# Attention outputs of seven tiles kept in device memory, and one output projection over all channels in the last tile

## Chip, cores and metric

The kernel runs on one core of a Trainium2 chip. The time is the device time of one execution in microseconds (us), from the first to the last instruction of the program with what lies around it. A core has five engines with a queue each: TensorE (PE), VectorE (DVE), ScalarE (ACT), GpSimd (POOL) and SyncE (SP). They run in order and wait for each other by semaphores. DMA queues move data between device memory and the on-chip memory (SBUF). Matmul results go to PSUM, eight banks of 512 f32 per partition.

## What is computed

One inference step of a two-layer encoder for 1024 prompt tokens and 8 x 16 sample tokens (1152 columns in all, `TOK`), model width 1024, in f32. Layer 0 mixes with differential attention (A, 4 heads) and windowed attention (B, 8 heads), layer 1 with a chunk band of 16 heads (C). Each mixer is followed by a gated conv FFN. What the change touches is the last line of each mixer, cut to it here:

```python
def even_mixer(h, pos, lam, lam_init, g_sub, sinks, w_in, w_out, cache):
    qa, ka, va, qb, kb, vb = split_even(h @ w_in)
    ...
    oa = rmsnorm(oa, g_sub) * (1 - lam_init)
    y = jnp.concatenate([oa.reshape(b, t, A_WIDTH), ob], axis=-1) @ w_out
    ...
def odd_mixer(h, pos, table, w_in, w_out, cache):
    ...
    return o @ w_out, (k_new, v_new)
```

and in the caller the gated residual: `x = x + gate * y`. `w_out` is 1024 x 1024, so y is a sum over 1024 attention channels.

## The kernel before

Activations lie transposed, channels on partitions: `xT` (the residual stream), `h` (normalized input, 8 slices of 128 channels x 1152) and `hl`, its low part. Every f32 product is made of three passes: high by high (f32r), high by low and low by high (bf16). `mm3` issues them for one block of columns, `mm9` for all 1152 columns in three blocks (`COLS`: 512, 512, 128), nine matmuls.

`attention` runs once per layer. It walks over **tiles** of 128 attention channels: tiles 0 to 3 are the heads of A and 4 to 7 those of B in layer 0, and 8 to 15 are C in layer 1. `T0` is a layer's first tile. A tile has 8 query blocks (units 0 to 7, with two score passes z), a drain (unit 8) and two groups of sample streams with cached keys.

`tile_steps` writes out the order of a tile as one list of steps, and every engine's `do` goes through the same list and issues its part of each step:
- KT, VT (transposes of k and v), CQ, CK, VS (splits of q, k, v into high and low), then for each unit S (scores, maxima, exponentials), T (transpose of the probabilities), V (product with v), N, O (the finished output, written by ACT to `actr` and by DVE to `actl`).
- F steps are filler for PE: one F is one `mm9` of the q, k or v projection of the *next* tile, eight of them per projection, 24 for three. A tile of B whose successor shares its keys has only the eight of q. The numbers in `body` are slots, and F steps are spread over them in proportion.
- OUT steps, eight a tile: step n multiplies `actr`/`actl` of the tile *before* by block n of `w_out` (`out_piece`, L1404) into banks 0 to 2, and DVE adds it, times the gate, to `xT` (`out_evac`, L1768; per step two of L1777, then L1783 and L1787). The next piece waits for that (`out_evac` semaphore), since it uses the same banks. They stand in units 0 and 1, which get no F steps. The last tile of a layer has OUT steps and no F; its own eight pieces come behind it.
- W splits weights: they come through `ring`, two slots of 128 x 1024. SP loads a chunk (`ring.load`, L162) once its slot's low part is made; ACT makes the high part (L169) and DVE the low part (L174) at a W step, which stands behind the end of a projection and prepares the chunk after next. The W behind v stands at the very end of a tile, ahead of the next VT.

In layer 0 all tiles are written out. In layer 1 the six tiles 9 to 14 are one loop (`Fori`, L1018). `act_free` lets ACT write `actr` again once the pieces of the tile before are evacuated. Behind a tile's KT and VT, PE also uses banks 3 and 4 (scores), 5 and 6 (transposes) and 7.

## Time and profile before

| | |
|---|---|
| median of 3 runs | 4500.71 us (4496.37 to 4506.84) |
| profiled execution, its own time | 4492.89 us |
| its span | 4491.3 us |
| mean granted TensorE clock | 0.899 |
| attention, layer 0 / layer 1 (first q copy to the last output) | 308.6 to 1361.6 / 2371.1 to 3515.0 us |
| HBM read / written | 250.80 / 51.56 MB |

A row of the windows view gives, for a stretch of the span, the busy time of each engine with the number of its instructions, the mean granted TensorE clock (1.00 is 2.4 GHz, 0.50 is 1.2 GHz), and the DMA engines' share and rate. A row of the timeline gives start, duration, engine, line, result and operands, and in brackets the idle time before it and who ended it. The busy time of PE counts modelled ends of matmuls and is not its peak rate. The windows of the tiles are cut where ACT starts to copy q (L1503, step CQ); an "opening" reaches from there to the first write of `actr`.

### The profile page before, as it was taken

The numbers are of one execution on the slowest core, as the hardware profiler recorded it, in microseconds if no ns is written. First come the engines' busy times: TensorE is split into PE (matmuls) and PEld (weight loads), VectorE is DVE, ScalarE is ACT, GpSimd is POOL, SyncE is SP. The second block draws the span as 40 slices with busy tenths as digits, with TensorE's granted clock in tenths as the row PEclk, the third lists the DMA queues.
The fourth block names the chain that finished last, engine by engine and source line by source line (L and its number), as shares of the span: only waits on it lengthen the run. The fifth ranks groups of instructions, "written<-read, shape, count | busy, mean of one in ns | idle before, by whom it ended". The sixth has DMA issues, their size and how long they took to land. (4 is left out here: it accounts for less than half of the span.)

```text
span 4491.3 us, 58536 instructions
## 1 busy us (share of the span) xinstructions
PE 3841.7 (86%) x21708; PEld 2211.7 (49%) x22097; DVE 2302.5 (51%) x3748; ACT 1365.6 (30%) x2652; POOL 466.2 (10%) x997
## 2 busy tenths in 40 slices
PE   6868887887867999999968888888888799999996
PEld 3535455544443555555535555555555355555553
DVE  4554555545446555555544555455544555555554
ACT  5533333333333122121223333333332321212212
POOL 0002122212110000000001111011110000000000
PEclk9887888878758999999988889999985799999998
DMA  7612122201001111111002232122321111111111
GB/s 297 239 46 58 41 60 73 58 23 44 21 17 43 39 43 43 38 43 40 27 24 86 86 98 91 50 79 93 98 76 36 39 43 43 39 39 43 43 34 43
DMA packets 200133, 277.97 MB, mean 62 GB/s; under 512 B 23984, under 2 KB 157721, under 8 KB 199286
## 3 DMA queue, kind: packets, MB, share of 16 engines
q1 hardware_dynamic: 170422, 164.42, 11.3%
q0 software_dynamic: 29504, 110.77, 8.2%
q8 instruction: 133, 2.18, 0.2%
q14 instruction: 74, 0.61, 0.0%
HBM read 250.80 MB, written 51.56 MB: 67 GB/s over the span
## 5 line engine op out<-in xcount | busy, mean ns | idle before, releaser
L95 PE MATMUL psum<-h,ffn_high 128*128 128x512 f32 (+1 forms) x2112 | 1036.9, 531 | 47.5 <-DVE hl L464 47.5
L97 PE MATMUL psum<-hl,ffn_high 128*128 128x512 bf16 (+1 forms) x2028 | 616.8, 337 | 0.0
L99 PE MATMUL psum<-h,ffn_low 128*128 128x512 bf16 (+1 forms) x2066 | 579.3, 332 | 2.9
L95 PE MATMUL psum<-actr,ffn_high 128*128 128x512 f32 (+1 forms) x1056 | 515.6, 528 | 56.5 <-DVE xT L482 40.8
L95 PEld LDWEIGHTS psum<-h,ffn_high 128*128 128x128 f32 x2112 | 409.7, 194 | 134.2 <-issue 43.6
L97 PEld LDWEIGHTS psum<-hl,ffn_high 128*128 128x128 bf16 x2112 | 206.4, 98 | 432.3 <-issue 373.4
L774 DVE TENSOR_SCALAR y<-u,cvT 128x1168 f32<-128x1168 f32 x88 | 78.2, 888 | 529.9 <-ACT u L725 529.9
L95 PE MATMUL psum<-h,attC_high 128*128 128x512 f32 (+1 forms) x576 | 288.4, 540 | 37.1 <-DVE hl L464 23.2
L97 PE MATMUL psum<-actl,ffn_high 128*128 128x512 bf16 (+1 forms) x1012 | 308.1, 337 | 0.0
L99 PE MATMUL psum<-actr,ffn_low 128*128 128x512 bf16 (+1 forms) x1034 | 290.3, 332 | 1.5
L95 PE MATMUL psum<-h,attAB_high 128*128 128x512 f32 (+1 forms) x480 | 262.9, 587 | 31.5 <-DVE hl L464 23.2
L169 ACT CAST ffn_high<-ffn_raw 128x1024 fp32r<-128x1024 f32 x132 | 138.8, 1054 | 478.0 <-PE psum L99 478.0
L95 PEld LDWEIGHTS psum<-actr,ffn_high 128*128 128x128 f32 x1056 | 205.2, 194 | 104.4 <-DVE xT L482 50.8
L719 ACT COPY u<-psum 128x1024 f32<-128x1024 f32 x88 | 89.3, 1014 | 546.9 <-PE psum L99 546.5
L482 DVE SCALAR_TENSOR_TENSOR xT<-psum,mod,xT 128x1024 f32<-128x1024 f32 x176 | 224.8, 1277 | 0.0
L1579 ACT ACTIVATE E_C<-psum,st_C 128x640 f32<-128x640 f32 (+3 forms) x144 | 97.3, 676 | 415.2 <-DVE st_C L1740 415.2
L97 PEld LDWEIGHTS psum<-actl,ffn_high 128*128 128x128 bf16 x1056 | 103.4, 98 | 212.6 <-issue 180.5
L1662 DVE TENSOR_TENSOR Wl_C<-psum,W_C 128x640 bf16<-128x640 f32 (+3 forms) x144 | 97.5, 677 | 196.6 <-ACT W_C L1533 196.0
L1579 ACT ACTIVATE E_AB<-psum,st_AB 128x256 f32<-128x256 f32 (+5 forms) x144 | 87.1, 605 | 361.3 <-DVE st_AB L1740 361.3
L593 POOL COPY so<-u 128x2 f32<-128x2 f32 x88 | 17.6, 200 | 1666.8 <-ACT u L720 1666.8
L1777 DVE SCALAR_TENSOR_TENSOR xT<-psum,mod,xT 128x512 f32<-128x512 f32 x256 | 181.7, 745 | 16.0 <-PE psum L87 15.3
L99 PEld LDWEIGHTS psum<-h,ffn_low 128*128 128x128 bf16 x2112 | 182.0, 100 | 0.0
(406 smaller groups left out, 8517.5 us busy)
## 6 DMA issues: line engine op xcount, KB each, us to landing
ada_raw<-in_ada_w SPq DMA_DIRECT2D x48, 1024.0 KB, 8.2
ffn_raw<-in_w_up SPq DMA_DIRECT2D x88, 512.0 KB, 4.0
ffn_raw<-in_w_down SPq DMA_DIRECT2D x44, 512.0 KB, 3.4
raw_C<-in_cache_c_k POOLq DMA_DIRECT2D x64, 256.0 KB, 6.2
raw_C<-in_cache_c_v POOLq DMA_DIRECT2D x64, 256.0 KB, 3.5
out_ck_s<-in_cache_c_k POOLq DMA_DIRECT2D x8, 1984.0 KB, 9.5
out_cv_s<-in_cache_c_v POOLq DMA_DIRECT2D x8, 1984.0 KB, 15.2
attC_raw<-in_w_in_odd SPq DMA_DIRECT2D x24, 512.0 KB, 3.9
```

The lines of the kernel that those rows point to most:

```text
L95: return pe.matmul(out, w, x[:, lo:hi], start=first and start, stop=last and stop, skip_group_check=True)
L97: return pe.matmul(out, top(w), xl[:, lo:hi], start=first and start, stop=last and stop, skip_group_check=True)
L99: return pe.matmul(out, wl, top(x[:, lo:hi]), start=first and start, stop=last and stop, skip_group_check=True)
L169: act.copy(self.w[s][:, :], self.raw[c % self.raws][:, :]).then_inc(self.high[s], 1)
L482: return dve.scalar_tensor_tensor(out=G.xT[:, n, 0:SEQ], in0=y[:, 0:SEQ], scalar=G.mod[:, a, 16 + n, 0:1], in1=G.xT[:, n, 0:SEQ], op0=ALU. ...
L593: pool.tensor_copy(so[:, 2 * g + j, 0:2], U[g][:, SEQ:SEQ + 2])
L719: act.copy(U[gate][:, 2:2 + SEQ], ps[:, 3 * gate:3 * gate + 2, :].rearrange("p b n -> p (b n)"))
L774: ch.then(dve.tensor_scalar(y[:, 0:n], u[:, 2:2 + n], cv[:, l, 2, bass.ds(f, 1)], cv[:, l, 3, bass.ds(f, 1)], ALU.mult, ALU.add))
L1579: i_ = act.activation(E[:, off:off + wd], s_banks[:, 0:wd], ACT.Exp, bias=nm[:, z:z + 1], scale=SCALE, accum_out=sm[:, z:z + 1])
L1662: i_ = dve.tensor_tensor(Wl[:, w0:w0 + wn], t_banks[:, 0:wn], W[:, w0:w0 + wn].bitcast(F32), ALU.subtract)
L1777: i_ = dve.scalar_tensor_tensor(out=x, in0=y, scalar=G.mod[:, a, 16 + n, 0:1], in1=x, op0=ALU.mult, op1=ALU.add)
```

## The change

- The OUT steps are gone. Once a tile of a layer (but the last) is done, SP writes `actr` and `actl` to device memory (`spill`: 128 x 1152 f32 and the same in bf16, two DMAs). It stands in SP's list behind the load of the q chunk of the tile after, and waits for the last `act_low` of its tile. ACT may write `actr` again once it has left (`act_free`).
- In the last tile (`TL`), when the last projection of the layer is done and `h` is free, SP reads the seven spilled tiles back into `h[:, 0..6]` and `hl[:, 0..6]` (`restore`, 14 DMAs). The last tile writes its own output to `h[:, 7]` (`act_of`).
- P steps (n, k), 56 of them, are the filler of the last tile from unit 3 on: `mm9` of slice k of `h` with block (k, n) of `w_out`, accumulated over k = 0 to 6 in banks 0 to 2. `w_out` comes by columns for these, eight loads. After k = 6 DVE adds the sum to `xT` by `residual`, the helper of the FFN (three instructions over 1152 columns); the next n waits for that.
- Behind the tile eight `mm9` with slice 7 and rows 896 to 1023 of `w_out` go to banks 0 to 2 and 3 to 5 by turns.
- The loop over tiles 9 to 14 is written out like the rest.
- `rtmp` gets its own SBUF place.

The diff, cut to its core:

```diff
-def tile_steps(kind, fill, out, keys):
+def tile_steps(kind, fill, last, keys):
...
-    steps = [("KT",), ("VT",), ("CQ",)] + outs[0:1] + [("CK",)] + outs[1:2] + [("VS",)] if keys else [("CQ",)] + outs[0:2]
+    steps = [("KT",), ("VT",), ("CQ",), ("CK",), ("VS",)] if keys else [("CQ",)]
...
-        one, two = ((outs[2:4], outs[4:5]), (outs[5:6], outs[6:8]))[u] if u < 2 and out else ([4], [4])
+        one, two = ([0], [0]) if last and u < 3 else ([4], [4])
...
+    todo = [("P", n, k) for n in range(KT) for k in range(KT - 1)] if last else \
+        [("F", name, k) for name in fill for k in range(KT)]
...
@@ sync, in do @@
-                if s == ("OUT", 0):
-                    row = (T - 1 - (8 if odd else 0)) * P
-                    ring.load(sp, c, w_out[bass.ds(row, P), :], turns)
+                if what == "P" and s[2] == KT - 2:
+                    ring.load(sp, c, w_out.rearrange("(k p) n -> p k n", p=P)[:, :, s[1] * P:(s[1] + 1) * P], 0,
+                              ("p (k n) -> p k n", dict(k=KT)))
+                    if s[1] == 1:
+                        spill(T - 1)
+                        restore()
...
                         ring.load(sp, c, src, turns, ("p (k n) -> p k n", dict(k=KT)))
+                    if s[1] == "q" and T > T0:
+                        spill(T - 1)
+
+            def spill(T):
+
+                t = T - T0
+                if T == TL - 1:
+                    sp.wait_ge(S.spilled, sb_ + 32 * t)
+                sp.wait_ge(S.act_low, un(T, UNITS - 1))
+                sp.dma_start(G.act_high_dram[t], actr[:, :].bitcast(F32)).then_inc(S.spilled, 16)
+                sp.dma_start(G.act_low_dram[t], actl[:, :]).then_inc(S.spilled, 16)
+
+            def restore():
+
+                ring.done(sp, cb + tiles[-1][3] - 1)
+                for t in range(7):
+                    if t == 6:
+                        sp.wait_ge(S.restored, sb_ + 32 * 6)
+                        sp.wait_ge(S.spilled, sb_ + 32 * 7)
+                    sp.dma_start(h[:, t, :].bitcast(F32), G.act_high_dram[t]).then_inc(S.restored, 16)
+                    sp.dma_start(hl[:, t, :], G.act_low_dram[t]).then_inc(S.restored, 16)
...
@@ tensor, in do @@
+                elif what == "P":
+                    j, k = s[1:]
+                    w, wl = ring.ready(pe, c) if k == 0 else (ring.w[c % 2][:, :], ring.wl[c % 2][:, :])
+                    if j == k == 0:
+                        pe.wait_ge(S.v_rows, n + 1)
+                        pe.wait_ge(S.q_evac, T + 1)
+                        pe.wait_ge(S.restored, sb_ + 32 * 6)
+                    elif k == 0:
+                        pe.wait_ge(S.out_evac, 2 * KT * odd + j)
+                    elif j == 0 and k == KT - 2:
+                        pe.wait_ge(S.restored, sb_ + 32 * 7)
+                    mm = mm9(pe, ps, 0, w[:, k * P:(k + 1) * P], wl[:, k * P:(k + 1) * P],
+                             h[:, k, :], hl[:, k, :], k == 0, k == KT - 2)
...
@@ scalar @@
             def act_free(T, c, turns):
-                act.wait_ge(S.out_evac, 3 * KT * T)
+                if T < TL:
+                    act.wait_ge(S.spilled, sb_ + 32 * (T - T0))
...
@@ vector, in do @@
-                elif what == "OUT":
-                    out_evac(T - 1, s[1], c, turns)
+                elif what == "P" and s[2] == KT - 2:
+                    ring.done(dve, c)
+                    residual(dve, ch, S, G, s[1], a, 0, rtmp[:, s[1] % 2, :]).then_inc(S.out_evac, 1)
```

**How the order moves.** First PE at the start of tile 9, the second tile of layer 1, before the change (L1292 the transposes of v, `actr_C`/`actl_C` the output of tile 8, the last row the first score):

```order
L1292 MATMUL psum<-consts,f_v_C 128x128 [waits v_evac]
L1292 MATMUL psum<-consts,f_v_C 128x128 x8
...
L85 MATMUL psum<-actr_C,attC_high 128x512 [waits v_rows,act_low]
L86 MATMUL psum<-actl_C,attC_high 128x512
L87 MATMUL psum<-actr_C,attC_low 128x512
...
L85 MATMUL psum<-actr_C,attC_high 128x512 [waits out_evac]
...
L85 MATMUL psum<-k_C,q_C 128x128 [waits exps]
```

and with the change, at the same place (`h` and `attC_high`: the first group of the projection for tile 10):

```order
L1313 MATMUL psum<-consts,f_v_C 128x128 [waits v_evac]
L1313 MATMUL psum<-consts,f_v_C 128x128 x8
L85 MATMUL psum<-k_C,q_C 128x128 [waits exps,k_low,q_low]
L86 MATMUL psum<-kl_C,q_C 128x128
L87 MATMUL psum<-k_C,ql_C 128x128
L95 MATMUL psum<-h,attC_high 128x512 [waits q_evac,v_rows,t_low1]
```

Two output pieces of nine matmuls stood between the transposes and the first score, and the filler of units 0 and 1 was output pieces. Now the score follows directly, and projections fill from unit 0 on.

Second, SP in layer 1 with the change, around the boundary of two tiles (`attC_raw<-in_w_in_odd` is the load of a q, k or v chunk, `act_high_dram<-actr_C` the spill):

```order
L162 DMA attC_raw<-in_w_in_odd 128x8x128 [waits t_low0]
L162 DMA attC_raw<-in_w_in_odd 128x8x128 [waits t_low1]
L1110 DMA act_high_dram<-actr_C 128x1152 [waits act_low]
L1111 DMA act_low_dram<-actl_C 128x1152
L162 DMA attC_raw<-in_w_in_odd 128x8x128 [waits t_low0]
```

Before the change the loads there are `w_out` and three times `w_in`, each with its slot's wait alone. Now the spill with its `act_low` stands between the loads of q (above it) and of k (below it).

Third, PE in unit 3 of tile 15 with the change (L1388: a transpose of probabilities):

```order
L1388 MATMUL psum<-consts,E_C 128x128 [waits w_low,exps]
L1388 MATMUL psum<-consts,E_C 128x128 x2
L95 MATMUL psum<-h,attC_high 128x512 [waits q_evac,restored,v_rows,t_low1]
L97 MATMUL psum<-hl,attC_high 128x512
```

Before the change nothing but attention stands there. Now the first P group does, and it waits for the restored slices.

## Rows read from the trace of the kernel before

**Rows 1.** Page, parts 1 and 2: busy time; granted clock in 40 slices.
```profile
PE 3841.7 (86%) x21708; PEld 2211.7 (49%) x22097; DVE 2302.5 (51%) x3748; ACT 1365.6 (30%) x2652; POOL 466.2 (10%) x997
...
PEclk9887888878758999999988889999985799999998
```

**Rows 2.** Windows: tile 8 (columns: busy us, count per engine, clock, DMA).
```profile
core 0: us, PE busy (x) PEld busy (x) DVE busy (x) ACT busy (x) POOL busy (x), PEclk, DMA share, GB/s
2371.10:2502.90 131.80, 113.08 (x726) 71.86 (x738) 57.57 (x120) 51.08 (x112) 22.13 (x43) 0.86 0.27 83
```

**Rows 3.** Windows: tiles 9 to 14 together.
```profile
2502.90:3351.40 848.50, 727.11 (x4782) 451.96 (x4860) 438.88 (x918) 302.03 (x668) 132.70 (x258) 0.92 0.26 81
```

**Rows 4.** Windows: tile 15, then its own output.
```profile
3351.40:3496.30 144.90, 112.09 (x572) 74.91 (x576) 68.34 (x147) 42.97 (x104) 22.27 (x43) 0.61 0.21 65
3496.30:3515.00 18.70, 16.68 (x70) 8.24 (x72) 15.16 (x34) 0.03 (x1) 0.00 (x0) 0.84 0.00 0
```

**Rows 5.** Windows: tile 0.
```profile
308.60:462.80 154.20, 125.65 (x652) 75.47 (x664) 64.20 (x126) 56.59 (x128) 32.48 (x56) 0.77 0.19 54
```

**Rows 6.** Windows: tiles 1 to 3 together.
```profile
462.80:924.70 461.90, 378.03 (x2170) 233.47 (x2208) 237.09 (x477) 166.94 (x382) 95.03 (x168) 0.87 0.20 57
```

**Rows 7.** Windows: tiles 4 to 6 together; tile 5 alone.
```profile
924.70:1252.50 327.80, 257.28 (x1417) 153.02 (x1443) 168.47 (x497) 108.24 (x375) 66.94 (x132) 0.78 0.11 31
...
1034.00:1144.40 110.40, 91.11 (x567) 54.17 (x577) 58.79 (x169) 37.16 (x125) 22.21 (x40) 0.90 0.12 35
```

**Rows 8.** Windows: tile 7, then its own output.
```profile
1252.50:1344.60 92.10, 65.06 (x342) 40.94 (x343) 45.84 (x153) 29.69 (x117) 11.74 (x28) 0.61 0.03 9
1344.60:1361.60 17.00, 15.69 (x70) 7.95 (x72) 14.34 (x32) 0.03 (x1) 0.00 (x0) 0.88 0.00 0
```

**Rows 9.** Windows: openings of tiles 8, 9, 0, 2; middle of tile 15.
```profile
2371.10:2393.20 22.10, 14.96 (x73) 7.66 (x76) 10.84 (x26) 9.94 (x25) 11.64 (x23) 0.85 0.86 289
2502.90:2536.20 33.30, 25.53 (x119) 13.28 (x121) 26.42 (x59) 9.52 (x24) 11.66 (x23) 0.90 0.63 203
308.60:332.40 23.80, 17.65 (x73) 8.84 (x76) 9.66 (x24) 10.47 (x25) 4.57 (x7) 0.76 0.20 55
617.70:648.50 30.80, 25.26 (x118) 12.94 (x121) 24.75 (x57) 10.07 (x25) 4.57 (x7) 0.89 0.17 46
3384.00:3458.40 74.40, 63.15 (x314) 43.78 (x316) 27.20 (x59) 22.52 (x60) 1.50 (x2) 0.50 0.01 4
```

**Rows 10.** Windows, line L95 alone (PE, weight loads): dense FFN.
```profile
1500.00:2200.00 700.00, 627.85 (x1287) 248.65 (x1287) 1.00 0.14 41
```

**Rows 11.** Timeline (start, us, instruction, idle before): boundaries 9-10 and 0-1.
```profile
2640.19 0.46 DVE L1698 TENSOR_TENSOR actl_C<-psum,actr_C 64x64 bf16<-64x64 f32 x2 [4.56 <-ACT actr_C L1609]
...
2642.41 1.05 ACT L169 CAST attC_high<-attC_raw 128x1024 fp32r<-128x1024 f32 x1
2645.22 1.12 ACT L1512 COPY sw_C<-psum 128x1152 f32<-128x1152 f32 x1 [1.76 <-PE psum L1292]
...
2642.77 1.20 PE L1303 MATMUL psum<-consts,f_k_C 128*128 128x128 f32 x9 [1.41 <-issue]
...
457.72 0.28 DVE L1688 SCALAR_TENSOR_TENSOR actl_AB<-psum,columns,actr_AB 128x64 bf16<-128x64 f32 x1 [3.41 <-ACT actr_AB L1565]
...
461.79 1.12 ACT L1512 COPY sw_AB<-psum 128x1152 f32<-128x1152 f32 x1 [3.18 <-PE psum L1292]
```

**Rows 12.** DMA issues: tensors, queue, count, KB each, median us to landing.
```profile
attC_raw<-in_w_in_odd SPq DMA_DIRECT2D x24, 512.0 KB, 3.9
...
attC_raw<-in_w_out_odd SPq DMA_DIRECT2D x8, 512.0 KB, 3.3
...
rope_AB<-in_rope SPq DMA_DIRECT2D x1, 1040.0 KB, 5.0
```

**Rows 13.** Line L1777: who waited for it (us in total, times).
```profile
  PEld psum L85: 103.2, 145
  PE psum L85: 74.0, 42
```

More of the change, by code:

```diff
@@ L849, in stream_width @@
     return P * (CACHE_B[kind] + 1)
-def tile_steps(kind, fill, out, keys):
-    outs = [("OUT", n) for n in range(KT)] if out else []
-    steps = [("KT",), ("VT",), ("CQ",)] + outs[0:1] + [("CK",)] + outs[1:2] + [("VS",)] if keys else [("CQ",)] + outs[0:2]
-    last = 0 if kind == "A" else 1
+def tile_steps(kind, fill, last, keys):
+    steps = [("KT",), ("VT",), ("CQ",), ("CK",), ("VS",)] if keys else [("CQ",)]
+    pair = 0 if kind == "A" else 1
     body = []
@@ L870, in tile_steps @@
         body += ([("S", u, 1)] if scored else []) + ([("O", u - 2)] if u > 1 else [])
-        body += ([("T", u - 1, 1)] if u and last else []) + two
+        body += ([("T", u - 1, 1)] if u and pair else []) + two
     body += [("V", QB - 1)]
@@ L881, in tile_steps @@
     total = sum(s for s in body if isinstance(s, int))
-    todo = [("F", name, k) for name in fill for k in range(KT)]
+    todo = [("P", n, k) for n in range(KT) for k in range(KT - 1)] if last else \
+        [("F", name, k) for name in fill for k in range(KT)]
     seen = sent = 0
@@ L903, in tile_steps, with unit_ends @@
     return steps + turn + later
+def unit_ends(s):
+    return s[0] == "F" and s[2] == KT - 1 or s[0] == "P" and s[2] == KT - 2
 def first_steps():
@@ L920, in plan @@
         out.append((k, T, fill, c))
-        c += len(fill) + (n > 0)
-    return out, c + 1
+        c += len(fill)
+    return out, c + KT + 1
 AB_CHUNKS = plan("AB")[1]
@@ L966, in attention @@
         cb = AB_CHUNKS if odd else 0
-        assert cb % 2 == 0
+        TL = tiles[0][1] + 7
+        sb_ = 2 * 16 * 7 * odd
         T0 = tiles[0][1]
@@ L1010, in run, with do_steps, act_of @@
         def run(eng, do):
-            do_steps(do, "A" if not odd else "C", T0 - 1, first_steps(), cb, 0)
-            if not odd:
-                for n, (kind, T, fill, c) in enumerate(tiles):
-                    do_steps(do, kind, T, tile_steps(kind, fill, n > 0, new_kv(kind, T)), cb + c, 0)
-            else:
-                do_steps(do, "C", T0, tile_steps("C", "qkv", False, True), cb + 3, 0)
-                with eng.Fori(T0 + 1, T0 + 7) as T:
-                    do_steps(do, "C", T, tile_steps("C", "qkv", True, True), cb + 6, 2 * (T - T0 - 1), loop=True)
-                do_steps(do, "C", T0 + 7, tile_steps("C", "", True, True), cb + 30, 0)
-        def do_steps(do, kind, T, steps, c, turns, loop=False):
-            if loop:
-                do("LOOP", kind, T, (0,), c, turns)
+            do_steps(do, "A" if not odd else "C", T0 - 1, first_steps(), cb)
+            for kind, T, fill, c in tiles:
+                do_steps(do, kind, T, tile_steps(kind, fill, T == TL, new_kv(kind, T)), cb + c)
+        def do_steps(do, kind, T, steps, c):
             for s in steps:
-                do(s[0], kind, T, s, c, turns)
-                if s == ("OUT", KT - 1) or s[0] == "F" and s[2] == KT - 1:
+                do(s[0], kind, T, s, c, 0)
+                if unit_ends(s):
                     c += 1
-            if loop:
-                do("END", kind, T, (0,), c, turns)
+        def act_of(T):
+            return (h[:, 7, :], hl[:, 7, :]) if T == TL else (actr[:, :], actl[:, :])
         def next_tile(kind, T):
@@ L1448, in _ @@
             run(pe, do)
+            w, wl = ring.ready(pe, cb + total - 1)
+            pe.wait_ge(S.act_low, un(TL, UNITS - 1))
             for n in range(KT):
-                out_piece(T0 + 7, n, cb + total - 1, 0)
+                pe.wait_ge(S.out_evac, 2 * KT * odd + (KT if n < 2 else KT + n - 1))
+                mm = mm9(pe, ps, 3 * (n % 2), w[:, n * P:(n + 1) * P], wl[:, n * P:(n + 1) * P],
+                         h[:, 7, :], hl[:, 7, :], True, True)
+                if n < KT - 1:
+                    mm.then_inc(S.out_ready, 1)
+            mm.then_inc(S.t_used[(cb + total - 1) % 2], 1)
         @block.scalar
@@ L1564, in do @@
                     lo = u * P if u < QB else SEQ + 64 * (u - QB)
-                    act.activation(actr[:, lo:lo + rows], ps[:, 7, 256:256 + rows], ACT.Copy,
+                    act.activation(act_of(T)[0][:, lo:lo + rows], ps[:, 7, 256:256 + rows], ACT.Copy,
                                    scale=G.gsub[:, 0:1] if kind == "A" else 1.0).then_inc(S.act_high, 1)
```

95 lines of the change are left out of this document (23 added, 72 removed).

## Prediction

> **What bounds the kernel now.** I read the page first: TensorE (PE) is busy 3841.7 us of 4491.3 (86%), and its granted clock moves between 0.5 and 1.0 of full speed [rows 1]. The change touches only the two attention stages, so I cut these by windows. A window runs from one ScalarE (ACT) copy of q to the next, which is one tile. Tile 8, the first of layer 1, has 24 filler groups (one k-slice of a q, k or v projection, nine matmuls, here "a group") and no output groups. It takes 131.8 us, PE busy 113.08, clock 0.86 [rows 2]. Tiles 9 to 14 carry eight output groups more and take 848.5 us, 141.4 each, at 0.92 [rows 3]. Tile 15 has the eight output groups and no projection to fill with: 144.9 us at clock 0.61, then 18.7 us for its own output [rows 4]. In layer 0, tile 0 (no output groups) takes 154.2 us, but tiles 1 to 3 with eight more groups take 461.9 us, 154.0 each [rows 5, 6]. Tiles 4 to 6 take 327.8 us, and tile 7 92.1 us at clock 0.61 and then 17.0 [rows 7, 8].
>
> So the tiles are near the PE bound but not on it: a chain of scores, maximum, exponential, transpose and product runs through PE, VectorE (DVE) and ACT, and groups fill its gaps. The last tile of each layer has no filler and a cold PE: 74.4 us of tile 15 are at 0.50 throughout [rows 9]. The change is about where the filler goes.
>
> **The price of one group.** From 1500 to 2200 us the FFN runs dense on PE at clock 1.00: 1287 matmuls of the first kind, three per group, in 700 us [rows 10]. That is 1.63 us a group. I use it for output groups too (same columns, same three passes).
>
> **Part 1: the output groups leave 12 tiles (1 to 6 and 9 to 14).** Tile 8 and tile 0 are what such a tile then looks like, because their lists of steps are the same.
> - Layer 1: 7 x 131.8 = 922.6 against 131.8 + 848.5 = 980.3, so -57.7, 9.6 a tile. The opening shows why: 22.1 us against 33.3 [rows 9]. It waits on DVE, whose 26.42 busy us fall to 10.84. The rest of the tile gives 1.6 back, at a lower clock.
> - Layer 0, tiles 1 to 3: the opening is 7.0 shorter in tile 0 (23.8 against 30.8) [rows 9], but the rest is 7 us longer, with the clock of the whole tile at 0.77 against 0.87 [rows 5, 6]. The bounds are 147 (the 7 us kept) and 154.2 (all given back). I take 152, nearer tile 0, since tile 8 too has the lower clock. 3 x 152 = 456.0 against 461.9: -5.9.
> - Tiles 4 to 6: no twin. The bounds are the two opening differences, 7.0 and 11.2; I take 10 each, because their middle waits on the chain and not on PE (257.28 busy of 327.8) [rows 7]: -30.
>
> **Part 2: the spill stands ahead of a weight load.** In the new order of SyncE (SP) both spill DMAs of tile T-1 are queued between the loads of the q and the k weights of tile T's filler, and the first of them waits for the last VectorE row of tile T-1. In the old order such a load waits only for a free slot. Who needs that k load? ACT splits exactly these weights at the boundary, ahead of the copy of v that opens the tile, and everything of the new tile stands behind it on ACT, then DVE and PE. Before: the last DVE row ends at 2640.65, ACT splits at 2642.41 and copies v at 2645.22 [rows 11]. After: the SP wakes at 2640.65, issues at about 0.37 us each, so the load leaves about 1 us later behind 885 KB of spill (128 x 1152 x 6 bytes). Extra bytes: the rope load brings 1040 KB in 5.0 us where 512 KB of full rows take 3.3, so 3.2 us per MB, 2.8 us for the spill; the w_in load itself takes 3.9 [rows 12]. It lands near 2640.65 + 1 + 2.8 + 3.9 = 2648.4 at worst, and 2645.6 if the spill delays nothing. I take 2647.6, as transfers overlap at their ends; plus the split's 1.05 us, v is copied at 2648.7, 3.5 us late. Bounds: 1.4 and 4.3. In layer 0 the boundary is shorter: the last DVE row ends at 458.00 and v is copied at 461.79, 3.8 us later and not 4.6 [rows 11], so 4.3 us. The boundary of tiles 4 to 5 opens with no v copy: 3. The boundary into the last tile is free of it, as its loads are ahead of the spill. Sum: layer 1, 6 x 3.5 = +21; layer 0, 4 x 4.3 up to tile 4 (0-1, 1-2, 2-3, 3-4) = +17.2, then 3 + 4.3 = +7.3. Total +45.5.
>
> The Trainium skill, DMA: Bandwidth & Descriptors, section Queues, rings and completion order, says that descriptors of one issuing engine's queue are consumed in ring order on each DMA engine. By that rule the load cannot pass the spill and the 3.5 stands; were the transfers independent, the bound of 1.4 would hold and the total be 25 us less. No row of this trace shows a load behind a spill.
>
> **Part 3: 56 groups go into the last tile of each layer.** No group can be placed before unit 3 there; seven k-slices for each of eight output chunks follow.
> - Tile 15: its own PE work is that of tiles 9 to 14 without their 32 groups: 727.11 / 6 = 121.2, less 32 x 1.63 = 52.2, so 69.0 us [rows 3]. Added 56 x 1.63 = 91.3, so 160.3 busy. Idle: tile 8 has 18.7 [rows 2]; +8 for the three units without filler (tile 8 has five groups there); +10 for seven chunk ends, since one accumulator must be cleared by DVE before the next chunk starts, for which PE waits at most (103.2 + 74.0) / 128 = 1.4 us per output group today [rows 13]; +3 for the restore of 5.3 MB beside the other transfers of the opening (203 GB/s over 33.3 us, 6.8 MB, in an opening of today; tile 8's reaches 289 [rows 9], so 6.8 + 6.2 MB need 45 us from the boundary, and the first group stands some 35 us behind it; bounds 0 and 10); -6 as denser filler covers more gaps. That is 34. 194 against 144.9: +49.1.
> - Tile 7: own work from tile 5, 91.11 - 52.2 = 38.9 [rows 7], + 91.3 = 130.2; idle 19.3 + 8 + 10 - 6 = 31. 161 against 92.1: +68.9.
> - After the tile: eight groups on two accumulators. today they take 17.0 and 18.7 us on one accumulator [rows 4, 8], with DVE busy 14.34 of the 17.0; two accumulators take PE's wait away but not DVE's work. I take 17.5 each: +0.5 and -1.2.
> The cold clock there does go (0.50 to about 0.9), and that is in the sum already: it is why 56 groups cost 49 us and not 91 in tile 15. In tile 7 they cost 69, because its chain is short and PE becomes the bound.
>
> **Part 4: the loop over tiles 9 to 14 becomes straight code.** All of layer 0 is straight today, and PE's wait at the loop's end is 1.41 us [rows 11], most of it beside ACT's copy. 0, at most -1.4 a tile.
>
> **Sum.** Layer 0: -5.9 - 30 + 17.2 + 7.3 + 68.9 + 0.5 = +58.0. Layer 1: -57.7 + 21 + 49.1 - 1.2 = +11.2. Together +69.2. The profiled execution took 4492.9, so 4562.1; the median of the three runs is 4500.7, 7.8 higher, and the same step from there is 4569.9. I forecast 4570.
>
> **The rivals.**
> A. The boundary wait is hidden (loads land early, or ACT had slack): 69.2 - 45.5, 4524. For: the load is ordered only one filler unit late. Against: ACT's split is the second row of the boundary [rows 11].
> B. Faster. Each output group costs its full 1.63 us in the 12 tiles, so 13.0 a tile, -156, and the boundary wait is hidden too. The last tiles keep the idle time they have now: +48 and +65, -0.7 for the ends. Sum -43.7: 4457. Its place is the clock: it needs tiles without output groups to run as warm as those with them. It decides once the saving passes 9.5 us a tile on the mean. Against: tile 0 is not shorter than tiles 1 to 3 at all [rows 5, 6].
> C. As B, but the boundary wait stays: -43.7 + 45.5 = +1.8, 4503, no change.
> D. The transfers hurt more: PE waits for the restored slices 12 us in each last tile and the bias and cache loads of the opening come late, 4600.
>
> **How the numbers follow.** Forecast 0.60, A 0.15, B 0.07, C 0.08, D 0.10. The range must hold 8 in 10: A, D and the forecast hold 0.85. Down from 4570: A's tiles at 147 (-15), boundary waits at 1.4 (-25), last tiles 10 each less (-20), together 4510; up: waits at 4.3 (+10), last tiles 10 more each, restore 10: 4610. I give 4508 to 4612. A measurement of this kernel tells 0.2% (9 us) from no change; faster by more is B, 0.07; within is C, 0.08; slower is the rest, 0.85.
>
> **What would show it.** Right: tiles 9 to 13 near 135 us, with an ACT split at each boundary that waits for attC_raw, ended by a DMA; tile 7 near 160 and tile 15 near 194 us, with a clock of 0.85 or more behind unit 3; DVE busy 170 us or more below today's 2302.5 [rows 1] without a shorter span. Wrong: tiles 1 to 3 under 145, or a v copy within 5 us of the last VectorE row of the tile before, or a tile 15 below 175.

## The result, and the profile after

The changed kernel takes **4560.6 us** in the median (4553.85 to 4575.45, four runs), the kernel before 4499.6 beside it. The ratio is 1.0142, interval 1.012 to 1.0164: slower by about 61 us. The forecast was 4570, in a range of 4508 to 4612. The profiled execution took 4553.85 us, 61.0 more than the one of before. Rows below have the columns of the rows of before.

The page, parts 1 and 2:

```profile
PE 3865.6 (85%) x21696; PEld 2214.6 (49%) x22097; DVE 2131.4 (47%) x3334; ACT 1369.5 (30%) x2654; POOL 467.9 (10%) x997
...
PEclk9887777767688999999989888888879899999998
```

VectorE lost 171 us of work (2302.5 in [rows 1]), and the kernel is slower all the same. Windows of tile 8, tiles 9 to 14, tile 15 and what follows it, then tile 0, tiles 1 to 3, tiles 4 to 6, tile 7 and what follows it (up to the FFN's first matmul):

```profile
core 0: us, PE busy (x) PEld busy (x) DVE busy (x) ACT busy (x) POOL busy (x), PEclk, DMA share, GB/s
2432.20:2565.80 133.60, 111.78 (x726) 70.77 (x738) 57.23 (x120) 51.12 (x113) 22.13 (x43) 0.87 0.29 89
2565.80:3376.00 810.20, 688.21 (x4356) 433.46 (x4428) 345.82 (x721) 298.63 (x662) 133.25 (x258) 0.85 0.28 88
3376.00:3551.20 175.20, 148.87 (x960) 90.05 (x977) 74.25 (x143) 48.67 (x111) 22.10 (x43) 0.88 0.33 106
3551.20:3579.00 27.80, 21.41 (x106) 10.35 (x106) 16.08 (x29) 1.25 (x3) 0.53 (x1) 0.94 0.01 2
307.80:465.60 157.80, 126.18 (x652) 75.66 (x664) 63.82 (x126) 56.49 (x128) 32.48 (x56) 0.76 0.20 55
465.60:943.40 477.80, 375.86 (x1956) 226.66 (x1992) 192.68 (x379) 165.96 (x380) 97.65 (x168) 0.75 0.20 57
943.40:1257.50 314.10, 223.67 (x1197) 135.71 (x1218) 122.39 (x399) 105.40 (x371) 65.83 (x132) 0.68 0.14 39
1257.50:1397.20 139.70, 119.97 (x737) 69.47 (x751) 51.76 (x149) 35.55 (x124) 11.59 (x28) 0.91 0.23 75
1397.20:1425.00 27.80, 21.44 (x105) 10.24 (x105) 16.08 (x29) 1.26 (x3) 0.52 (x1) 0.94 0.00 1
```

Read against [rows 2 to 8]. Tiles 9 to 14 are 38.3 us shorter (810.2 for 848.5) and tiles 4 to 6 are 13.7 shorter. Tiles 1 to 3 are 15.9 *longer*, at clock 0.75 for 0.87. Tile 15 grew by 30.3 us and tile 7 by 47.6. What follows them grew by 7.5 and 8.5: to the FFN's first matmul it was 20.3 and 19.3 us before. All in all layer 0 is 61.9 us longer and layer 1 1.3 us longer; what lies outside the two stages is 2.2 us shorter.

The boundary of tiles 9 and 10, where [rows 11] showed the old one (last VectorE row, SyncE's queue, ScalarE):

```profile
2697.46 0.46 DVE L1710 TENSOR_TENSOR actl_C<-psum,actr_C 64x64 bf16<-64x64 f32 x2 [1.58 <-ACT actr_C L1625]
...
2697.94 0.34 SPq L1110 DMA_DIRECT2D act_high_dram<-actr_C  x1
...
2698.33 0.42 SPq L1111 DMA_DIRECT2D act_low_dram<-actl_C  x1
2698.80 1.94 SPq L162 DMA_DIRECT2D attC_raw<-in_w_in_odd  x2
...
2700.09 1.12 ACT L1506 COPY f_v_C<-psum 128x1152 f32<-128x1152 f32 x1 [2.66 <-PE psum L99]
...
2704.28 1.04 ACT L169 CAST attC_high<-attC_raw 128x1024 fp32r<-128x1024 f32 x1 [3.06 <-DMA attC_raw<-in_w_in_odd]
2705.23 1.11 ACT L1527 COPY sw_C<-psum 128x1152 f32<-128x1152 f32 x1
```

This is the wait of Part 2 as it was put. The last VectorE row ends at 2697.92, SyncE wakes and issues two spills and then the load, and ScalarE's split stands 3.06 us until the load has landed. Before, the split followed ScalarE's copy at once. The v copy comes 7.3 us after the VectorE row, before 4.6. Who ScalarE waited for (us, times, longest), first over layer 1 and then over layer 0, and the DMA issues of after:

```profile
ACT attC_high L169 <- DMA attC_raw<-in_w_in_odd: 17.6, 6, 3.2
...
ACT attAB_high L169 <- DMA attAB_raw<-in_w_in_even: 38.8, 5, 10.7
```

```profile
attC_raw<-in_w_in_odd SPq DMA_DIRECT2D x24, 512.0 KB, 5.1
...
h<-act_high_dram SPq DMA_DIRECT2D x14, 576.0 KB, 7.6
...
act_high_dram<-actr_C SPq DMA_DIRECT2D x7, 576.0 KB, 2.8
...
act_low_dram<-actl_C SPq DMA_DIRECT2D x7, 288.0 KB, 3.8
```

The same loads took 3.9 us before [rows 12]. From the last VectorE row to the q copy, the twelve boundaries at which a load stands behind the spill (0-1 to 5-6 and 8-9 to 13-14) grew by 30.9 us in layer 0 and 14.4 in layer 1, 45.3 together; 45.5 was forecast.

### The profile page after: what moved, and what is told of

Same layout as the page of the kernel before. It is cut to its first block and busy times, and to the rows that moved or that the text cites. A ratio compares the mean times of both kernels' runs of the same rounds, so it can differ in the third digit from the quotient of the medians.

```text
span 4552.3 us, 55845 instructions
## 1 busy us (share of the span) xinstructions
PE 3865.6 (85%) x21696; PEld 2214.6 (49%) x22097; DVE 2131.4 (47%) x3334; ACT 1369.5 (30%) x2654; POOL 467.9 (10%) x997
## 5 line engine op out<-in xcount | busy, mean ns | idle before, releaser
L95 PE MATMUL psum<-h,ffn_high 128*128 128x512 f32 (+1 forms) x2112 | 1036.9, 531 | 47.5 <-DVE hl L464 47.3
L95 PE MATMUL psum<-actr,ffn_high 128*128 128x512 f32 (+1 forms) x1056 | 515.7, 529 | 56.4 <-DVE xT L482 40.7
L95 PEld LDWEIGHTS psum<-h,ffn_high 128*128 128x128 f32 x2112 | 409.7, 194 | 134.2 <-issue 43.6
L95 PE MATMUL psum<-h,attC_high 128*128 128x512 f32 (+1 forms) x768 | 404.4, 566 | 31.7 <-DVE hl L464 23.2
L95 PE MATMUL psum<-h,attAB_high 128*128 128x512 f32 (+1 forms) x672 | 372.9, 594 | 35.4 <-DVE hl L464 23.1
L169 ACT CAST ffn_high<-ffn_raw 128x1024 fp32r<-128x1024 f32 x132 | 138.9, 1055 | 478.0 <-PE psum L99 478.0
L482 DVE SCALAR_TENSOR_TENSOR xT<-psum,mod,xT 128x1024 f32<-128x1024 f32 x208 | 265.7, 1277 | 0.0
L95 PEld LDWEIGHTS psum<-actr,ffn_high 128*128 128x128 f32 x1056 | 205.2, 194 | 104.3 <-DVE xT L482 50.8
L99 PE MATMUL psum<-h,attC_low 128*128 128x512 bf16 (+1 forms) x752 | 232.6, 365 | 1.4 <-issue 0.7
L97 PE MATMUL psum<-hl,attC_high 128*128 128x512 bf16 (+1 forms) x691 | 233.1, 365 | 0.0
L97 PE MATMUL psum<-hl,attAB_high 128*128 128x512 bf16 (+1 forms) x615 | 219.0, 386 | 0.0
L99 PE MATMUL psum<-h,attAB_low 128*128 128x512 bf16 (+1 forms) x643 | 208.4, 379 | 2.3 <-issue 1.0
L85 PE MATMUL psum<-k_AB,q_AB 64*128 64x256 f32 (+2 forms) x160 | 86.3, 540 | 136.3 <-issue 45.8
```

The source lines that it names most:

```text
L85: pe.matmul(out, w, x, start=start, stop=False, skip_group_check=True)
L95: return pe.matmul(out, w, x[:, lo:hi], start=first and start, stop=last and stop, skip_group_check=True)
L97: return pe.matmul(out, top(w), xl[:, lo:hi], start=first and start, stop=last and stop, skip_group_check=True)
L99: return pe.matmul(out, wl, top(x[:, lo:hi]), start=first and start, stop=last and stop, skip_group_check=True)
L169: act.copy(self.w[s][:, :], self.raw[c % self.raws][:, :]).then_inc(self.high[s], 1)
L482: return dve.scalar_tensor_tensor(out=G.xT[:, n, 0:SEQ], in0=y[:, 0:SEQ], scalar=G.mod[:, a, 16 + n, 0:1], in1=G.xT[:, n, 0:SEQ], op0=ALU. ...
```

## Experiments

In each the times are medians beside those of the kernel before on the same chip. "After" is the changed kernel (4560.6, ratio 1.0142). A name like e1 in brackets stands for the run in the rest of the text.

**The boundary wait** (e1). The spill one load later:

```diff
                         ring.load(sp, c, src, turns, ("p (k n) -> p k n", dict(k=KT)))
+                    spill_held()
                     if s[1] == "q" and T > T0:
-                        spill(T - 1)
+                        held.append(T - 1)
```

> The changed kernel, but each spill is issued one weight load later on SyncE: the k chunk that ScalarE splits at the tile's end is now loaded ahead of the spill, and the load of the chunk after that stands behind it. Theory (the boundary wait is a queueing wait): the 45.3 us by which the times from the last VectorE row of a tile to the q copy grew in 12 boundaries (30.9 in layer 0, 14.4 in layer 1) go, and the split stops waiting for a DMA; 4560.6 - 45.3 = 4515, between 4505 and 4525. Rival 1 (the wait only moves: ScalarE may write actr again only when the spill is out, and that is later now): tile lengths grow in their middle by what the boundary gives, 4545 or more. Rival 2 (TensorE is warmer for the wait: a cold clock gives it back): the boundary gains 45 but the tiles get 15 to 25 us longer in sum at a lower clock, 4530 to 4540.

Measured: 4519.2 beside 4498.4, ratio 1.0039 (1.0021 to 1.0057). That is 41 us less than after (46 by the ratios), inside the theory's 4505 to 4525. ScalarE at the same boundary, then tiles 1 to 3, 4 to 6 and 8 to 14:

```profile
2664.36 1.12 ACT L1514 COPY f_v_C<-psum 128x1152 f32<-128x1152 f32 x1 [2.66 <-PE psum L99]
2665.38 1.05 ACT L169 CAST attC_high<-attC_raw 128x1024 fp32r<-128x1024 f32 x1
2667.57 1.12 ACT L1535 COPY sw_C<-psum 128x1152 f32<-128x1152 f32 x1 [1.15 <-PE psum L1321]
```

```profile
463.40:924.10 460.70, 369.23 (x1992) 223.56 (x1992) 192.48 (x378) 165.83 (x379) 97.70 (x168) 0.78 0.22 60
924.10:1225.90 301.80, 230.76 (x1218) 139.94 (x1218) 122.80 (x398) 105.98 (x372) 65.91 (x132) 0.66 0.14 40
2402.70:3335.60 932.90, 810.11 (x5166) 507.06 (x5166) 403.14 (x840) 349.74 (x772) 155.01 (x301) 0.85 0.28 89
```

The split has no wait in brackets. Nothing waits for the later spill, so rival 1 falls; the tiles give nothing back, so rival 2 falls too.

Next (e9), the wait kept and only the load put ahead of the spill's bytes:

```diff
+                    if held:
+                        sp.wait_ge(S.act_low, un(held[-1], UNITS - 1))
                     if nk == "B" and s[1] != "q":
...
                         ring.load(sp, c, src, turns, ("p (k n) -> p k n", dict(k=KT)))
+                    spill_held()
```

> The changed kernel with the k load issued ahead of the spill, but behind the same wait for the last VectorE row of the tile (e1_load_first took it out from behind the wait too). It splits the 41 us that e1_load_first gained into the wait and the bytes of the spill. In the changed kernel the wait ends, the spill is issued 0.03 us later and the load 0.89 us later, which lands 5.2 to 5.5 us after its issue in layer 1; with few bytes ahead it landed in 3.9. Theory (the load queues behind the spill's bytes and leaves after its issues): it lands 2.4 us earlier, and the gap ahead of ScalarE's split falls from 2.8-3.2 to 0.4-0.8 us in layer 1 and from 6.3 to about 3.9 in the boundaries 0-1, 1-2 and 3-4; 12 boundaries x 2.4 = 29 of the 41 us, 4526 to 4538. Rival 1 (the spill's bytes cost nothing, only the wait counts): the gap shrinks by the 0.9 us of the two issues, 11 us, 4545 to 4555. Rival 2 (the wait costs nothing without the bytes ahead): as e1_load_first, 4515 to 4522.

Measured: 4548.5 beside 4492.7, ratio 1.0109 (1.0074 to 1.0143). The boundary 9-10 (SyncE, then ScalarE), and the sum of the waits in layer 1:

```profile
2700.70 0.37 SPq L162 DMA_DIRECT2D attC_raw<-in_w_in_odd  x1
2701.12 0.57 SPq L1120 DMA_DIRECT2D act_high_dram<-actr_C  x1
```

```profile
2705.27 1.04 ACT L169 CAST attC_high<-attC_raw 128x1024 fp32r<-128x1024 f32 x1 [1.34 <-DMA attC_raw<-in_w_in_odd]
```

```profile
ACT attC_high L169 <- DMA attC_raw<-in_w_in_odd: 7.3, 6, 1.4
```

The load now lands 4.5 us after its issue (3.9 alone, 5.4 behind the spill), and the gap falls by 1.7 us, not by the 2.4 expected. Over the boundaries the trace gives 25 us back (14.4 in layer 0, 10.3 in layer 1), the medians 12 with runs 15 us apart. The time lies inside rival 1's 4545 to 4555 and misses the theory's 4526 to 4538, but rival 1's reason (the bytes cost nothing) does not hold at the boundary: its gap should have fallen by 0.9 us and fell by 1.7. What is shown: both parts count. At boundary 9-10 the bytes ahead cost the load 0.9 us and the two issues 0.9. The wait for the last row costs the rest, some 20 of the 45 us by the traces. The Trainium skill, DMA: Bandwidth & Descriptors, section Queues, rings and completion order, has descriptors consumed in ring order on each DMA engine. The load behind the spill is late, as that says; but a load ahead of it (and of the next load, issued 1.5 us later) is late by 0.6 us too, so order is not all that it depends on.

**Part 1 alone** (e5), without spills and without groups in the last tiles:

```diff
-    todo = [("P", n, k) for n in range(KT) for k in range(KT - 1)] if last else \
-        [("F", name, k) for name in fill for k in range(KT)]
+    todo = [("F", name, k) for name in fill for k in range(KT)]
...
-                    if s[1] == "q" and T > T0:
-                        spill(T - 1)
...
```

> The changed kernel without the 56 filler groups of the last tiles, without spill and restore; it leaves out seven eighths of each output projection (only the slice of the last tile is multiplied). It is Part 1 alone: tiles 1 to 6 and 9 to 14 without output groups and without a boundary wait. By the prediction tiles 1 to 3 are 152 us, tiles 4 to 6 are 99.3 in the mean and tiles 9 to 14 131.8 each, together 93.6 less than before. By the trace of the changed kernel with its boundary waits taken off: tiles 1 to 3 154.8, tiles 4 to 6 99.8, tiles 8 to 14 132.8, together 76.5 less. The last tiles lose their eight output groups too: between 0 (the chain bounds them) and 2 x 8 x 2.73 = 44 us less. So 4499.6 - 76.5 - 0 to 44 = 4380 to 4423. Rival (the tiles get faster the more is taken, as the clock is no function of the output groups): tiles 1 to 3 at 147 or less and tiles 9 to 14 at 128, a total under 4380. Whether the clock of tiles 1 to 3 stays at 0.75 with no wait at all decides between a clock that the wait lowered and one that the missing groups lowered.

Measured: 4404.7 (two runs, 4399.1 and 4410.2) beside 4498.4, inside the expected 4380 to 4423. Tiles 1 to 3, 4 to 6 and 8 to 14:

```profile
462.90:923.60 460.70, 369.21 (x1992) 223.56 (x1992) 192.49 (x378) 165.59 (x379) 97.70 (x168) 0.78 0.20 54
923.60:1224.90 301.30, 231.36 (x1218) 140.00 (x1218) 121.57 (x397) 104.98 (x371) 65.89 (x132) 0.66 0.10 27
2333.80:3266.00 932.20, 811.74 (x5166) 511.54 (x5166) 402.27 (x839) 349.21 (x772) 155.56 (x301) 0.84 0.26 81
```

Against 461.9, 327.8 and 980.3 before: -1.2, -26.5 and -48.1, together -75.8. The lengths are those of e1 within 0.7 us, with no boundary wait in either. The low clock of tiles 1 to 3 (0.78 here, 0.75 after, 0.87 before) is thus for the most part not the wait's doing.

**The loop alone written out** (e4) in the kernel before:

```diff
-                do_steps(do, "C", T0, tile_steps("C", "qkv", False, True), cb + 3, 0)
-                with eng.Fori(T0 + 1, T0 + 7) as T:
-                    do_steps(do, "C", T, tile_steps("C", "qkv", True, True), cb + 6, 2 * (T - T0 - 1), loop=True)
...
+                for n, (kind, T, fill, c) in enumerate(tiles):
+                    do_steps(do, kind, T, tile_steps(kind, fill, n > 0, new_kv(kind, T)), cb + c, 0)
```

> The kernel before, with nothing changed but the loop over tiles 9 to 14 written out as straight code (Part 4 of the prediction). Theory: nothing to 1.4 us a tile, so 4491 to 4500 beside 4499.6. Rival: the branch and the registers of the loop cost more than the profile shows, and part of what tiles 9 to 14 gained is theirs: 15 us or more, under 4485. A second rival: straight code costs instruction fetches, up to 10 us slower, 4510.

Measured: 4509.5 beside 4498.4, ratio 1.0029 (1.0013 to 1.0045), eleven us *slower*; the second rival gave the size. Tiles 9 to 14; then the last stretch of tile 12 (from the end of unit 7's output) in this kernel and, in the second fence, before:

```profile
2499.90:3368.90 869.00, 766.33 (x4860) 478.14 (x4860) 440.15 (x918) 301.59 (x667) 133.60 (x258) 0.87 0.25 79
...
3032.10:3078.80 46.70, 40.69 (x264) 26.23 (x263) 18.58 (x35) 16.78 (x29) 9.01 (x18) 0.85 0.25 74
```

```profile
3023.50:3066.20 42.70, 34.74 (x260) 22.26 (x262) 18.59 (x35) 16.88 (x30) 9.01 (x18) 1.00 0.29 89
```

The same instructions with the same ScalarE and VectorE times take 4.0 us more, and what differs is the granted clock, 0.85 for 1.00. Tile 12 is the plainest case: over the six tiles this stretch took 42.4 to 45.4 us at 0.92 to 1.00 in the loop, and 46.3 to 47.8 at 0.82 to 0.85 in straight code. Tiles 9 to 14 of this trace are 20.5 us longer than before (869.0 for 848.5), more than the medians' eleven. The second rival's reason finds no support: no instruction fetch shows up as a wait, and the instruction queues moved 2.5 MB here and 2.8 before. Why the clock falls into another pattern when the loop's branch is gone was not found.

**Who sets the openings** (e7): before, with VectorE's evacuation of a piece cut to one column:

```diff
+                    if not (isinstance(T, int) and T == T0 + 7):
+                        x = x[:, 0:1]
+                        dve.tensor_tensor(x, y[:, 0:1], x, ALU.add).then_inc(S.out_evac, 1)
+                        continue
```

> The kernel before, but VectorE adds only one column of each output piece to xT (it leaves out the residual add of attention in all tiles but the layer's last own output); TensorE does all its work. It tells who sets the openings of 33.3 us (tiles 9 to 14) and 30.7 (tiles 1 to 3) that the prediction put down to VectorE. Theory (VectorE's evacuation bounds them): they fall by 7 to 11 us, to near tile 8's 22.1 and tile 0's 23.8, with the output groups still there; the rest of the tile keeps its length or its clock falls a little; 12 tiles x 7 to 9, 4395 to 4415. Rival (the nine matmuls of each output piece bound them): openings within 3 us of now, 4465 to 4498.

Measured: 4431.4 (two runs, 4424.6 and 4438.2) beside 4497.6, between the two. The openings of tiles 10 and 1:

```profile
2601.10:2630.40 29.30, 23.62 (x119) 12.42 (x121) 14.86 (x51) 9.51 (x24) 11.64 (x23) 0.94 0.71 229
459.40:485.00 25.60, 22.20 (x119) 11.87 (x121) 13.75 (x49) 10.20 (x26) 4.57 (x7) 1.00 0.22 60
```

VectorE's 26.4 us fall to 14.9, yet the opening falls only from 33.3 to 29.3. Of the 11.2 us that part it from tile 8's, 4.0 go with VectorE's work and 7.2 stay with the groups. In tile 1 VectorE's work is worth 5.0 us (30.6 to 25.6).

**Why did tiles 1 to 3 gain nothing?** First (e8), eight groups that nobody waits for put back into each of the twelve tiles:

```diff
+                    elif T0 < T < TL:
+                        for _ in range(zeros(nk, nT, name, k)):
+                            mm9(pe, ps[0:96], 0, Z[:, :], top(Z[:, :]), h[:, k, :], hl[:, k, :], False, False)
...
```

> The changed kernel with eight more groups of nine matmuls in each of tiles 1 to 6 and 9 to 14, right behind filler groups; their weights are zeros on 96 columns, added to a running sum, so nothing changes in the results. The 13 us of TensorE work that the change took out of each tile are back as work that nobody waits for. Theory (with output groups gone the clock of tiles 1 to 3 fell from 0.87 to 0.75, and the work taken out was mostly given back by it): tiles 1 to 3 grow by 0 to 5 each at a clock of 0.83 or more, tiles 4 to 6 by 2 to 8 each, tiles 9 to 14 by 5 to 10 each; 45 to 95 us in all, 4605 to 4655. Rival 1 (TensorE work adds up at its price whatever the clock): 13 a tile, 156 in all, 4717. Rival 2 (tiles 1 to 3 are held by the chain alone and the clock has no part in it): they grow by 0 to 5 with the clock still under 0.80.

Measured: 4680.0 beside 4497.6, 119 more than after. Tiles 1 to 3, 4 to 6 and 9 to 14:

```profile
465.00:969.80 504.80, 399.54 (x2172) 245.92 (x2208) 192.66 (x379) 165.02 (x379) 95.13 (x168) 0.80 0.19 54
969.80:1311.30 341.50, 252.68 (x1412) 155.43 (x1434) 122.09 (x399) 105.03 (x371) 65.84 (x132) 0.76 0.13 36
2619.90:3501.60 881.70, 758.07 (x4788) 483.31 (x4860) 346.60 (x721) 296.84 (x662) 132.68 (x258) 0.85 0.26 80
```

Tiles 1 to 3 grew by 9.0 each at a clock of 0.80, tiles 4 to 6 by 9.1, tiles 9 to 14 by 11.9. The theory that missing *work* had cooled TensorE, and that work put back would be nearly free, falls: here a group costs 1.1 to 1.5 us, while the 24 output groups of tiles 1 to 3, in units 0 and 1, left for a gain of 1.2 us. But with them gone the projection groups moved forward into units 0 and 1 as well. The next kernel (e3) is e1 with their place restored, the groups of the twelve tiles kept out of units 0 and 1:

```diff
-        one, two = ([0], [0]) if last and u < 3 else ([4], [4])
+        one, two = ([0], [0]) if (last and u < 3) or (late and not last and u < 2) else ([4], [4])
```

> e1_load_first (spill one load later) with one more edit: tiles 1 to 6 and 9 to 14 put no filler group into units 0 and 1, so the same groups stand in units 2 to 8 and in the sample streams, as they did before the change; units 0 and 1 have no filler at all. It asks why the 8 groups that left tiles 1 to 3 gave nothing, while 8 idle groups put back (e8_zero_groups) cost 9 us a tile. Theory (placement: the removed groups had stood where TensorE waits for others anyway; spread over units 0 to 8 the remaining ones leave the middle thinner and colder, 0.76 against 0.91 in units 2 and 3): openings stay at 20 to 22 us, the rest of the tile comes back to the lengths of before, 123 us in tiles 1 to 3 and 107 to 109 in tiles 9 to 14; tiles 1 to 3 near 145 (153.6 in e1), tiles 9 to 14 near 129 (133.6), in all 45 to 60 us under e1_load_first, 4460 to 4475. Rival (the clock of the middle needs the output groups ahead of it, wherever the filler stands): the middle stays at 0.76 to 0.80, the opening is colder still, tiles 1 to 3 at 152 to 160, 4510 to 4540.

Measured: 4502.3 beside 4496.5, ratio 1.0014 (0.9995 to 1.0033), 17 us under e1 (11 by the ratios), between the ranges of theory (4460 to 4475) and rival (4510 to 4540). Tile 1 from its second to its fourth output, in the kernel before, after, with the groups put back, and with the groups late (one fence each):

```profile
501.90:520.60 18.70, 16.82 (x95) 9.94 (x96) 8.55 (x20) 7.56 (x21) 1.09 (x2) 0.91 0.00 1
```

```profile
498.40:520.00 21.60, 17.13 (x86) 10.21 (x87) 9.84 (x21) 9.52 (x22) 3.13 (x6) 0.76 0.11 27
```

```profile
502.40:524.00 21.60, 17.65 (x95) 10.84 (x96) 9.78 (x22) 9.45 (x23) 3.13 (x6) 0.84 0.11 27
```

```profile
492.40:511.10 18.70, 16.84 (x95) 10.12 (x96) 8.55 (x20) 7.54 (x22) 1.09 (x2) 0.91 0.00 1
```

Late groups bring back the 18.7 us and the 0.91 of before, with no output group in the tile. Tiles 1 to 3 take 438.3 us (460.7 in e1), 145 to 147 each, as expected. This answers the question. The output groups were not cheap: with the filler in the same late place, tiles 1 to 3 take 461.9 us with them (455.3 to 458.9 in the three kernels e4, e2 and e10, whose layer 0 is that of before) and 438.3 without, 17 to 24 us for 24 groups, 0.7 to 1.0 each and near e8's 1.1. The filler that moved into units 0 and 1 took 22.4 us of it back. In layer 1 the theory fails: tiles 10 to 14 take 136.5 each, 3 more than in e1. Their opening, without any group, was expected at 20 to 22 us:

```profile
2648.40:2672.90 24.50, 12.28 (x48) 6.44 (x49) 10.93 (x26) 8.59 (x23) 11.64 (x23) 0.58 0.86 272
```

It takes 24.5 at clock 0.58, and the end of the tile, from unit 7's output on, is at 0.82 (47.8 us, for 42.4 at 1.00 in tile 10 before). That end is slow in the straight code of e4 too (46.5 us in its tile 10), so it can't be put down to the late filler alone. Why late filler helps in layer 0 and costs 3 us a tile in layer 1 stays open (e10, below, has that too). The Trainium skill, TensorE: Matmul & The Clock Gate, section HAM oscillation — how this bites in real kernels, says that idle gaps between bursts of matmuls send the clock down. The opening's 12.3 busy us of 24.5 at 0.58 agree; that a tile's length hangs on where the gaps lie, with equal work, is what these two kernels add.

**The restore** left out (e6):

```diff
                         spill(T - 1)
-                        restore()
...
-                        pe.wait_ge(S.restored, sb_ + 32 * 6)
...
```

> The changed kernel without the restore: no slices come back, and the output projection multiplies what stands in h, so it leaves out the use of the spilled outputs and nothing of the work on the engines. Theory (as the trace of after reads): the opening of tile 15, 28.0 us against 21.7 of tile 8, falls to 22, that of tile 7 stays; the first groups of the last tiles wait for nothing: 6 to 9 us less, 4552 to 4555. Rival D of the prediction (the restore costs 12 us in each last tile): 24 us less, 4537. Rival (it costs nothing, as the opening is long from the bias loads alone): within 3 us of 4560.6 and an opening of 28.

Measured: 4562.6 (4539.9 to 4569.7) beside 4498.4, which the medians can't tell from after; the profiled execution was the fastest of the four. The profiles can: the opening of tile 15 and the whole tile, then the opening after,

```profile
3368.90:3391.60 22.70, 9.11 (x31) 4.55 (x31) 10.94 (x26) 8.57 (x24) 11.64 (x23) 0.57 0.88 290
3368.90:3536.70 167.80, 147.10 (x978) 89.32 (x979) 74.35 (x143) 48.73 (x111) 22.14 (x43) 0.91 0.24 75
```

```profile
3376.00:3404.00 28.00, 9.10 (x31) 4.55 (x31) 10.93 (x26) 8.64 (x24) 11.62 (x23) 0.56 1.02 366
```

The opening is 5.3 us shorter without the restore. The tile is 7.4 us shorter than the 175.2 of after, and 4.8 shorter than the 172.6 of a kernel below (e2) that has the restore too. So the restore costs 5 to 7 us in tile 15, and nothing in tile 7, which is unchanged (139.8). Rival D of the prediction, 12 us in each, falls; so does the rival here that put the long opening down to the bias loads alone.

**A version from it** (e2). Layer 0 as before, layer 1 as changed with the spill late. The old OUT steps stand beside the new ones, and the layer chooses:

```diff
-def tile_steps(kind, fill, last, keys):
+def tile_steps(kind, fill, last, keys, out=False):
...
+        early = not odd
...
+                if s == ("OUT", 0):
+                    row = (T - 1) * P
+                    ring.load(sp, c, w_out[row:row + P, :])
...
-                    if s[1] == "q" and T > T0:
-                        spill(T - 1)
+                    spill_held()
+                    if s[1] == "q" and T > T0 and not early:
+                        held.append(T - 1)
```

> Layer 0 as before the change (output pieces of the tile before, no spill), layer 1 as changed but with each spill one weight load later; tiles 9 to 14 straight. With the spill issued later the attention of layer 0 took 1182.7 us against 1153.1 before (29.6 more) and that of layer 1 1224.0 against 1233.5 (9.5 less), from the first sum over ones to the FFN's first. Theory (the two layers are independent, and the change pays only where a tile's chain is long): 4498.4 - 9.5 = 4489, between 4481 and 4494, with tile 15 near 175 and tiles 8 to 14 at 932 in sum. Rival (layer 1's gain is within what the clock moves from run to run, and nothing is left over several rounds): 4495 to 4505.

Measured: **4478.9 beside 4497.6, ratio 0.996 (0.9943 to 0.9976)**, 0.4% under the kernel before, and 2 us below the range expected. Its profiled execution took 4488.6. Tiles 8 to 14 and tile 15, and tiles 1 to 3 with layer 0 as before:

```profile
2367.70:3309.90 942.20, 814.30 (x5082) 512.04 (x5166) 403.34 (x840) 350.01 (x773) 155.59 (x301) 0.84 0.29 88
3309.90:3482.50 172.60, 146.04 (x960) 89.11 (x977) 74.33 (x143) 48.77 (x111) 22.15 (x43) 0.89 0.33 107
465.80:922.70 456.90, 375.22 (x2170) 231.17 (x2208) 236.92 (x477) 166.92 (x382) 95.41 (x168) 0.88 0.21 57
```

The first two are 38.1 us under the 980.3 of before and 27.7 over the 144.9. The third is 5.0 us under the 461.9 of before with the same order of work: one trace tells the length of three tiles only to some 5 us. With the late groups of e3 in tiles 9 to 14 on top (e10):

```diff
-        one, two = ([0], [0]) if last and u < 3 else ([4], [4])
+        one, two = ([0], [0]) if (last and u < 3) or (late and not last and u < 2) else ([4], [4])
```

> e2_layer1_only (layer 0 as before the change, layer 1 changed with the spill one load later; 4478.9 against 4497.6) with the edit of e3_late_fill in tiles 9 to 14 alone. Theory (placement): tiles 9 to 14 go from 134.0 in the mean to 128 to 130, 24 to 36 us less, 4443 to 4455. Rival: nothing or slower, 4475 to 4500.

Measured: 4492.1 beside 4496.5, ratio 0.9992 (0.9975 to 1.0009): the rival. Tiles 10 to 14 are 136.5 each again, as in e3, for 134.3 in e2.

## The prediction, step by step

| term | forecast | measured | from |
|---|---|---|---|
| Part 1, tiles 1 to 3 | -5.9 | -1.2 | e5 |
| Part 1, tiles 4 to 6 | -30 | -26.5 | e5 |
| Part 1, tiles 9 to 14 | -57.7 | -48.1 | e5, tiles 8 to 14 |
| Part 2, layer 0 / layer 1 | +24.5 / +21 | +30.9 / +14.4 | trace of after; e1: 41 in all |
| Part 3, tile 7 and its end | +69.4 | +56.1 | windows |
| Part 3, tile 15 and its end | +47.9 | +37.8 | windows |
| Part 4 | 0 | +11 (20.5 in its trace) | e4, inside Part 1's -48.1 |
| sum | +69.2 | +63.4 (profiled pair +61.0) | |

The forecast was right in sign, and its size within 10 us of the median. Part of that is luck: Part 1 saved 17.8 us less than put down, and Part 3 cost 23.4 less.

- **Part 1.** Tile 8 is a good twin and tile 0 a better one, though tile 8, with one and the same order of steps, took 131.0 (e1) to 138.9 us (e9) over these kernels. Tile 0's 154.2 came out, at 153.6 a tile in e5; my choice of 152, between bounds, had no row behind it. What made it a twin is that its filler too stands in units 0 and 1; with late filler the tiles take 146.1 (e3), near the bound of 147 that I set aside. The sentence that the opening "waits on DVE" holds for 4.0 us of 11.2 (e7). In layer 1 the miss may be Part 4's: against the straight code of e4 (tiles 8 to 14: 131.6 + 869.0 = 1000.6) the groups' leaving saved 68.4, 11.4 a tile in six and more than the forecast 9.6. That straight code costs the same once the output groups are gone is not shown.
- **Part 2.** The mechanism is shown by e1. The sizes were off in both layers and cancelled. In layer 1 the load landed 6.3 us behind the last VectorE row and not 7.0. In layer 0 two boundaries are dearer (2-3 by 6.2 us, 4-5 by 9.2): there the load is that of a B key, which comes in two halves one after the other, the second issued only when the first has landed, after the wait. Boundary 5-6 grew by 5.5 us, where the load is one of `w_out` by columns and landed 6.7 us after its issue. The prediction priced all boundaries up to 3-4 alike and 4-5 lower, and missed this.
- **Part 3.** TensorE's work was sized well. About 53 of the 56 groups ran inside the tile and 3 behind it, so with 5.4 us for these tile 7 has 125.4 us busy for 130.2 and tile 15 154.3 for 160.3. The idle term was too large, 19.7 for 31 and 26.3 for 34. In tile 15 most of the miss is the +10 for the chunk ends. PE's waits there, in tile 15 and in tile 7:

```profile
  DVE xT L482: 2.9, 2
```

```profile
  DVE xT L482: 6.6, 6
```

  In tile 15 PE waited at two of the seven chunk ends; that attention steps stood between chunks at the others is how I read it. In tile 7 it waited at six, 1.1 us each, near the 1.4 forecast; the rest of its miss lies in the +8 and the -6, which no run parts. The restore was put at +3 within 0 and 10, and is 5 to 7. Behind the tiles the forecast of 17.5 us each (+0.5 and -1.2) was too low: it is 8.5 and 7.5 us more than before, 5.4 of them the three groups that did not fit into the tile. So Part 3 is 40.1 us too high inside the two tiles and 16.7 too low behind them.
- **Part 4.** Its bounds (0 to -1.4 a tile) had only one side. Straight code was slower, at a lower granted clock, which no row of before could show; the cause of the lower clock is open.
- **Rivals.** A fell: the split had no slack. B and C asked that a tile without output groups run as warm as one with them; tiles 1 to 3 fell from 0.87 to 0.75. Tiles 9 to 14 fell from 0.92 to 0.85, but the straight code had them at 0.87 with output groups still there (e4), and they gave 11.4 us each against it, near B's 13. On the mean the saving was 6.3 us a tile (75.8 in twelve), under the 9.5 at which B would have decided. D fell with e6.

Of the signs named: tiles 9 to 13 took 135.9 us in the mean ("near 135"), tile 7 139.7 and tile 15 175.2 (160 and 194 were said, both high, and a tile 15 below 175 was named as a sign of being wrong); ScalarE's split waited, ended by a DMA; VectorE fell by 171 us.
